# Seven half-size products for eight in an MLP down projection, and a place for each piece of w_mod

## What is computed

```python
m = jax.nn.silu(c) @ w_mod + b_mod            # (1024) @ (1024, 6*1024): shifts, scales, gates sh1, sc1, g1, sh2, sc2, g2
h = rmsnorm(x, g_attn) * (1.0 + sc1) + sh1    # the context tokens likewise, from c_ctx
...
x = x + g1 * (mix @ w_out)
h = rmsnorm(x, g_mlp) * (1.0 + sc2) + sh2     # (1024 tokens, 1024)
a = jax.nn.relu(h @ w_mlp1)                   # w_mlp1 (1024, 4096): the up product
x = x + g2 * ((a * a) @ w_mlp2)               # w_mlp2 (4096, 1024): the down product
```

## Time and profile before

| what | value |
|---|---|
| median of 3 runs | 1471.31 us (1468.08 to 1471.95) |
| profiled execution, own time | 1470.41 us |
| its span, and granted clock | 1468.6 us, 0.984 |
| TensorE, VectorE, ScalarE, GpSimd busy | 96%, 57%, 42%, 27% |
| chain that ended last | TensorE 77%, VectorE 10%, ScalarE 8%, DMA 2% |

### The profile page before, as it was taken

The page is one execution under the profiler, slowest core; times in us unless marked ns, Lnnn a source line. Parts: engine busy times, 40 slices in busy tenths (PEclk is TensorE's granted clock), DMA queues, the critical chain, the costliest instruction groups (busy, mean ns, idle before and its releaser), DMA issues.

```text
span 1468.6 us, 19191 instructions
## 1 busy us (share of the span) xinstructions
PE 1403.3 (96%) x7466; PEld 1184.4 (81%) x7466; DVE 837.4 (57%) x1183; ACT 610.7 (42%) x1195; POOL 390.5 (27%) x263
## 2 busy tenths in 40 slices
PE   4799998899999999999999999999999999999998
PEld 0588887788788998988888888888888888888887
DVE  0677787788887877775775344352433524344342
ACT  1565655777777777972223121130301203021120
POOL 1465654000099991501101111020101102011010
PEclk7799998999999999999999999999999999999999
DMA  8546647900156546201132011020201102021113
GB/s 315 195 125 173 177 145 232 305 18 1 35 179 205 183 125 182 67 1 58 44 101 73 28 58 58 29 86 0 86 29 57 57 29 86 0 80 34 33 40 115
DMA packets 117203, 141.04 MB, mean 96 GB/s; under 512 B 7928, under 2 KB 98936, under 8 KB 114320
## 3 DMA queue, kind: packets, MB, share of 16 engines
q1 hardware_dynamic: 116880, 140.08, 30.5%
q0 software_dynamic: 256, 0.05, 0.0%
HBM read 108.37 MB, written 31.74 MB: 95 GB/s over the span
## 4 chain that ended last, share of the span: by engine, by line
PE 77%; DVE 10%; ACT 8%; DMA 2%; issue 2%; POOL 0%; SPq 0%; DVEq 0%; ACTq 0%; POOLq 0%
PE f_ps L2080 23%; PE f_ps L2073 22%; PE a_ps L1378 7%; PE o_ps L1733 6%; PE a_ps L1394 5%; PE a_ps L1422 4%; PE t_ps L940 3%; ACT s_pr L1473 2%; ACT s_pT L1483 2%; PE t_ps L929 2%; DVE s_nmx L1556 1%; PE t_ps L955 1%; DMA t_wm<-in_w_mod 1%; ACT l_pr L1490 1%; DVE l_nb L1561 1%
## 5 line engine op out<-in xcount | busy, mean ns | idle before, releaser
L2080 PE MATMUL f_ps<-f_w,f_aT 128*128 128x512 f32 x1536 | 351.8, 390 | 0.7
L2080 PEld LDWEIGHTS f_ps<-f_w,f_aT 128*128 128x128 f32 x1536 | 287.7, 188 | 63.5 <-DVE mix L2056 3.6
L2073 PE MATMUL f_ps<-h,f_w 128*128 128x512 f32 x1440 | 327.8, 389 | 0.5 <-DVE f_w L1931 0.5
L2073 PEld LDWEIGHTS f_ps<-h,f_w 128*128 128x128 f32 x1440 | 270.2, 188 | 56.9 <-DVE f_w L1931 0.9
L1983 POOL TENSOR_TENSOR f_w2r<-f_w2r,f_g 128x1024 f32<-128x1024 f32 x32 | 81.0, 2531 | 604.4 <-DMA f_w2r<-in_w_mlp 604.4
L2056 DVE TENSOR_TENSOR mix<-mix,f_ps 128x512 f32<-128x512 f32 x112 | 72.0, 684 | 205.2 <-PE f_ps L2080 204.7
L2037 DVE TENSOR_TENSOR f_a<-f_r 128x1024 f32<-128x1024 f32 x32 | 59.6, 1864 | 183.8 <-ACT f_r L2013 183.8
L2000 ACT ACTIVATE f_w<-f_w2r 128x1024 fp32r<-128x1024 f32 x32 | 33.7, 1054 | 292.7 <-PE f_ps L2080 285.0
L1570 DVE TENSOR_TENSOR l_pT<-a_ps,l_pT 128x512 fp32r<-128x512 f32 (+1 forms) x192 | 109.0, 594 | 53.0 <-ACT l_pT L1483 52.9
L1378 PE MATMUL a_ps<-l_k,l_q 96*128 96x512 f32 (+1 forms) x576 | 136.5, 366 | 0.5 <-DVE l_mo L1591 0.5
L2013 ACT ACTIVATE f_r<-f_ps 128x1024 f32<-128x1024 f32 x32 | 32.9, 1029 | 228.3 <-PE f_ps L2073 219.6
(11 more groups left out here) (199 smaller groups left out, 1896.1 us busy)
## 6 DMA issues: line engine op xcount, KB each, us to landing
l_wg<-in_w_mod SPq DMA_DIRECT2D x8, 2048.0 KB, 8.1
f_w1r<-in_w_mlp SPq DMA_DIRECT2D x32, 512.0 KB, 4.1
f_w2r<-in_w_mlp SPq DMA_DIRECT2D x32, 512.0 KB, 4.5
t_wm<-in_w_mod SPq DMA_DIRECT2D x8, 1024.0 KB, 7.5
scratch_k<-t_kT SPq DMA_DIRECT2D x20, 384.0 KB, 4.5
l_k<-scratch_k SPq DMA_DIRECT2D x8, 960.0 KB, 10.1
scratch_q<-t_qT SPq DMA_DIRECT2D x16, 384.0 KB, 4.8
l_q<-scratch_q SPq DMA_DIRECT2D x8, 768.0 KB, 6.7
```

The lines of the kernel that those rows point to most:

```text
L2073: last = nc.tensor.matmul(ps[:, b + half, :], w1[:, slot, w, k, :], h2[x][:, k, half * BANK:(half + 1) * BANK], start=(k == 0 and i == 0), ...
L2080: last = nc.tensor.matmul(ps[:, DB[t % 2] + half, :], aT[x][:, f, t * P:(t + 1) * P], w2[w][:, f, half * BANK:(half + 1) * BANK], start=(f ...
```

## The change

**The down product.** A turn's product of 512 hidden columns is cut into halves along the tokens (rows, 512 each), the hidden columns and the output columns. Instead of the eight products of halves it makes seven, by the scheme of Strassen and Winograd, and takes sums and differences of halves as operands:

- VectorE forms two row sums of a (`row_sums`) and two differences (`difference`); GpSimd forms four differences of the gated w2 (`mix_weights`); ScalarE and VectorE split each of the 14 operands (`high`, `low`). Each of these works on 2 x 512 elements per partition.
- A product is four token tiles t of 2 x 3 matmuls (`product`). M1, M6, M7 and M4 go on in the same banks 4 to 7, M2 and then M5 and M3 in banks 0 and 1, two tiles each. After each tile `take` adds the bank to a region of `mix`: 28 additions a turn, for 16.
- The operands have two sets of buffers, so the split of a product waits until the one before the last is done (`free`). In the last turn there are three sets more, in the room that the up products leave.
- The up products are single halves of 24 matmuls (`up_next`), one between products, for the turn after. `a` has two buffers. ScalarE squares in place, and VectorE no longer squares. w2 is loaded in two pieces of 1 MB a turn. The loop is unrolled.

**The token stage.** Each of the 8 pieces of w_mod has a place of its own, `ident` is loaded ahead of them, and the first product no longer waits for it. The w_in weights `a0` wait for the first four products, since they are written over that place. x tile 1 is loaded and squared ahead of `a1`, and scaled ahead of the low part of w_kv; tile 2 is scaled earlier; `uq` is split in token tile 1 instead of 2.

```diff
-    WR = 3
-    wm = Z.room("L")("t_wm", [P, WR, 2 * D])
+    wm_in = {i: Z.room(at, skip)(f"t_wm{i}", [P, n, 2 * D]) for i, at, skip, n in ((0, "H", 0, 4), (4, "L", 0, 3), (7, "T", 9984, 1))}
+    wm = [wm_in[i][:, k - i, :] for k in range(KC) for i in (0, 4, 7) if 0 <= k - i < (4, 0, 0, 0, 3, 0, 0, 1)[i]]
...
         def load_wm(k):
-            if k >= WR:
-                sp.wait_ge(wm_used, k - WR + 1)
-            sp.dma_start(wm[:, k % WR, :], A["w_mod"][0, k * P:(k + 1) * P, 0:2 * D]).then_inc(wm_loaded[k % WR], 16)
+            sp.dma_start(wm[k], A["w_mod"][0, k * P:(k + 1) * P, 0:2 * D]).then_inc(wm_loaded[k], 16)
 
         def next_x(i):
             sp.wait_ge(emptied, slot["x1", i] + 1)
             load_x(i + 2)
 
         sp.dma_start(cc[:, :, :], A["c_cols"]).then_inc(c_loaded, 16)
-        for k in range(WR):
-            load_wm(k)
         sp.dma_start(ident[:, :], A["ident"]).then_inc(ident_loaded, 16)
-        for k in range(WR, KC - 2):
+        for k in range(KC - 2):
             load_wm(k)
         load_x(0)
         load_wm(KC - 2)
         load_wm(KC - 1)
         load_raw("a0")
+        load_x(1)
         load_raw("a1")
-        load_x(1)
...
+            if j == "a0":
+                act.wait_ge(wm_used, 4)
...
         high_weights("a0")
+        square_x(1, stx[:, 1:2])
         high_weights("a1")
         hi_fill("x0", 0)
         hi_fill("x1", 0)
-        square_x(1, stx[:, 1:2])
...
+        inverse_x(1)
         low_weights("a1")
-        inverse_x(1)
+        scale_x(1)
...
-        pe.wait_ge(ident_loaded, 16)
         pe.wait_ge(silu_ready, 1)
         for k in range(KC):
-            pe.wait_ge(wm_loaded[k % WR], 16 * (k // WR + 1))
+            pe.wait_ge(wm_loaded[k], 16)
             for j in range(4):
-                last = MM(ps[32 * j:32 * j + 32, UB, :], silu[:, k, :], wm[:, k % WR, j * BANK:(j + 1) * BANK],
+                last = MM(ps[32 * j:32 * j + 32, UB, :], silu[:, k, :], wm[k][:, j * BANK:(j + 1) * BANK],
                           start=(k == 0), stop=(k == KC - 1))
             last.then_inc(wm_used, 1)
+        pe.wait_ge(ident_loaded, 16)
...
+    UPB, XB, YB = (2, 4), 4, 0
+    M1, M2, M6, M5, M3, M7, M4 = range(7)
...
+    ROW, HIGH_D = {M1: 0, M2: 0, M6: 0, M5: 1, M3: 0, M7: 1, M4: 1}, {M1: 0, M2: 0, M6: 1, M5: 1, M3: 1, M7: 1, M4: 0}
+    bank_of = lambda i, t: XB + t if i in (M1, M6, M7, M4) else YB + t % 2
+    region_of = lambda i, t: (4 * ROW[i] + t, HIGH_D[i])
+    number = lambda d, i, t: NG * d + GROUPS.index((i, t))
+    ORDER = [(0, 0), (1, 0), (0, 1), (1, 1), (2, 0), (2, 1), (3, 0), (3, 1)]
...
+    def load_w2(d, fh):
+        if d:
+            sp.wait_ge(b_low, 7 * (d - 1) + (M4 if fh else M7) + 1)
+        f = 2 * fh
+        sp.dma_start(w2[:, f:f + 2, :], w2_dram[:, FC * d + f:FC * d + f + 2, :]).then_inc(w2_loaded[fh], 16)
...
+    def slot(d, i):
+        if d == NCH - 1:
+            return (1, 0, 2, 3, 4, 1, 0)[i]
+        return (7 * d + i) % 2
+
+    def free(eng, d, i):
+        if d == NCH - 1 and i in (M6, M5, M3):
+            eng.wait_ge(up_ready, 2 * NF)
+        elif d == NCH - 1 and i > M3:
+            eng.wait_ge(out_ready, NG * d + DONE[M1 if i == M7 else M2])
+        elif 7 * d + i > 1:
+            before = 7 * d + i - 2
+            eng.wait_ge(out_ready, NG * (before // 7) + DONE[before % 7])
...
+        load_w2(0, 0)
+        load_w2(0, 1)
+        for g in range(2, 6):
             load_w1(g)
+        for c in range(1, NCH):
+            load_w1(FC * c + 2)
+            load_w1(FC * c + 3)
+            if c < NCH - 1:
+                load_w1(FC * c + 4)
+            load_w2(c, 0)
+            if c < NCH - 1:
+                load_w1(FC * c + 5)
+            load_w2(c, 1)
...
+        def mix_weights(d):
+            made = 4 * d
+            pool.wait_ge(w2_gated, FC * d + 4)
+            pool.wait_ge(b_low, 7 * d + M1 + 1)
+            G.tensor_tensor(b_part(0, 0), b_part(0, 1), b_part(0, 0), ALU.subtract).then_inc(w2_mixed, 1)
+            pool.wait_ge(w2_mixed, made + 1)
+            free(pool, d, M6)
+            t2 = op_b[slot(d, M6)][2][:, :, :]
+            G.tensor_tensor(t2, b_part(1, 1), b_part(0, 0), ALU.subtract).then_inc(w2_mixed, 1)
+            pool.wait_ge(w2_mixed, made + 2)
+            pool.wait_ge(b_low, 7 * d + M2 + 1)
+            G.tensor_tensor(b_part(1, 0), b_part(1, 0), t2, ALU.subtract).then_inc(w2_mixed, 1)
+            G.tensor_tensor(b_part(0, 1), b_part(1, 1), b_part(0, 1), ALU.subtract).then_inc(w2_mixed, 1)
...
+        def w1_high(g):
             act.wait_ge(w1_loaded, g * 16 + 16)
...
+            act.wait_ge(up_ready, 2 * g - 2 if g > 3 else g + 1)
+            nc.scalar.activation(w1[:, g % 2, 0, :, :], w1r[:, :, :], ACT.Copy).then_inc(w1_hi, 1)
+
+        def rectify(c, n, f, half, b):
+            x = a[c % 2][:, f, half * HB:(half + 1) * HB]
+            act.wait_ge(up_ready, 8 * c + n + 1)
+            if n == 0 and c > 1:
+                act.wait_ge(a_low, 7 * (c - 1))
+            nc.scalar.activation(x, ps[:, b, :], ACT.Relu).then_inc(rect, 1)
+            act.wait_ge(rect, 8 * c + n + 1)
+            nc.scalar.activation(x, x, ACT.Square).then_inc(a_ready, 1)
+
+        def high(d, i):
+            s = slot(d, i)
+            free(act, d, i)
+            if i in HALF:
+                act.wait_ge(a_ready, 8 * d + 8)
+            else:
+                act.wait_ge(a_mixed, 4 * d + {M5: 1, M6: 2, M3: 3, M7: 4}[i])
+            nc.scalar.activation(op_a[s][0][:, :, :], a_source(d, i), ACT.Copy).then_inc(a_hi, 1)
+            if i in (M1, M2, M3):
+                act.wait_ge(w2_gated, FC * d + (2 if i == M1 else 4))
+            else:
+                act.wait_ge(w2_mixed, 4 * d + {M5: 1, M6: 2, M4: 3, M7: 4}[i])
+            nc.scalar.activation(op_b[s][0][:, :, :], b_source(d, i), ACT.Copy).then_inc(b_hi, 1)
+
+        for n, (f, half) in enumerate(ORDER):
+            if f == 2 and half == 0:
+                w1_high(2)
+                w1_high(3)
+            if f == 3 and half == 0:
+                w1_high(4)
+            rectify(0, n, f, half, UPB[f % 2] + half)
+        high(0, M1)
...
+        def row_sums(d):
+            dve.wait_ge(a_ready, 8 * d + 8)
+            dve.wait_ge(a_low, 7 * d + M1 + 1)
+            s1, s2 = a_part(d, 0, 1), a_part(d, 0, 0)
+            V.tensor_tensor(s1, s1, a_part(d, 1, 1), ALU.add).then_inc(a_mixed, 1)
+            dve.wait_ge(a_mixed, 4 * d + 1)
+            V.tensor_tensor(s2, s1, s2, ALU.subtract).then_inc(a_mixed, 1)
+
+        def difference(d, i):
+            free(dve, d, i)
+            dve.wait_ge(a_mixed, 4 * d + 2)
+            V.tensor_tensor(a_source(d, i), a_part(d, 1, 0 if i == M3 else 1), a_part(d, 0, 0), ALU.subtract).then_inc(a_mixed, 1)
+
+        def take(d, i, *tiles):
+            for t in tiles:
+                row, half = region_of(i, t)
+                n = number(d, i, t)
+                dve.wait_ge(out_ready, n + 1)
+                if (row, half) in written:
+                    dve.wait_ge(added, written[row, half])
+                x = acc[:, 4 * half:4 * half + 4, row * P:(row + 1) * P]
+                y = fin[:, 2 * row + half, :].rearrange("p (k c) -> p k c", c=P) if d == NCH - 1 and i in (M2, M3, M7, M4) else x
+                V.tensor_tensor(y, x, ps[:, bank_of(i, t), :].rearrange("p (k c) -> p k c", c=P), ALU.add).then_inc(added, 1)
+                written[row, half] = n + 1
...
+        w1_low(2)
+        w1_low(3)
+        w1_low(4)
+        low(0, M1)
+        for c in range(1, NCH):
+            d = c - 1
+            low(d, M2)
+            w1_low(FC * c + 1)
+            row_sums(d)
+            take(d, M1, 0, 1, 2, 3)
+            low(d, M6)
+            take(d, M2, 0, 1)
+            w1_low(FC * c + 2)
+            take(d, M2, 2, 3)
+            low(d, M5)
+            take(d, M6, 0, 1, 2, 3)
+            difference(d, M3)
+            low(d, M3)
+            take(d, M5, 0, 1)
+            w1_low(FC * c + 3)
+            take(d, M3, 0, 1)
+            take(d, M5, 2, 3)
+            difference(d, M7)
+            low(d, M7)
+            if c < NCH - 1:
+                w1_low(FC * c + 4)
+            take(d, M3, 2, 3)
+            low(d, M4)
+            take(d, M7, 0, 1, 2, 3)
+            low(c, M1)
+            take(d, M4, 0, 1, 2, 3)
+        d = NCH - 1
+        low(d, M2)
+        row_sums(d)
+        low(d, M6)
+        take(d, M1, 0, 1, 2, 3)
+        low(d, M5)
+        take(d, M2, 0, 1)
+        difference(d, M3)
+        low(d, M3)
+        take(d, M2, 2, 3)
+        difference(d, M7)
+        take(d, M6, 0, 1, 2, 3)
+        low(d, M7)
+        take(d, M5, 0, 1)
+        low(d, M4)
+        take(d, M3, 0, 1)
+        take(d, M5, 2, 3)
+        take(d, M3, 2, 3)
+        take(d, M7, 0, 1, 2, 3)
+        take(d, M4, 0, 1, 2, 3)
...
+        def product(d, i, *tiles):
+            s = slot(d, i)
+            pe.wait_ge(a_low, 7 * d + i + 1)
```

(40 more changed lines are left out.)

327 lines of the change are left out of this document (149 added, 178 removed).

## The result

The changed kernel takes **1435.6 us** (median of 4 runs, 1433.8 to 1439.2) against 1469.7 us (1467.8 to 1472.0) for the kernel before on the same chip: a ratio of 0.9771, 95% interval 0.9749 to 0.9793. The forecast was 1437 us, the range 1421 to 1457. The profiled execution has a span of 1434.3 us and took 1436.1 itself, so 34.3 us of span are to be explained.

The account below looks back on a forecast made before the run. The prediction took TensorE, busy 96% of the span, as the bound, so fewer MLP matmuls save time if operands are ready. Terms from -43.5 us for removed matmuls to +17 for the last turn sum to -34.1: 1437 us, range 1421 to 1457.

Parts of the forecast that it names:

- waits at the heads of turns: MLP, head of each turn: the down product's waits for additions into mix should go, -3.5 us.
- MLP start, stand: Start of the MLP: w1's third block stands behind four pairs of Relu and Square, so TensorE waits 3.5 us; +3.0 us.
- MLP start, clock: Start of the MLP: the clock may fall in the stand; about half of 2.7 us taken, +1.5 us.
- seven middle turns: MLP turns with up products: these cover the extra work, M2's bank free 1.6 to 3.4 us ahead; 0 us.
- last turn, waits: Last MLP turn, no up products: TensorE stands 12 to 13 us at M2's third tile, about 3 later; +17 us.
- last turn, clock: Last MLP turn: after the long stand the clock is lost, 2.7 us partly under VectorE's work; +2 us.
- token stage and what follows: Token stage: earlier w_mod -5.3 us, earlier x tile 1 scaling -2.7, clock kept -2; -10 us, bounds 5 to 14.
- the exclusion of VectorE and GpSimd: Shared SBUF port lock: the two engines exclude each other, PSUM reads aren't held; last turn 6.7 us longer.
- B: Rival: the last turn doesn't stall, so 19 us of stand and clock come back; 1418 us, chance 0.13.
- C: Rival: M2's third tile is late 2 to 3 us in each of seven turns; 1451 to 1458 us, chance 0.17.
- D: Rival: M2's third tile stands 4.3 us and loses 2.7 of clock in seven turns; 1486 us, chance 0.07.
- E: Rival: the token stage gives little, its earlier modulation absorbed by tables and weights; 1447 us, chance 0.15.

Follow-up runs that it names:

- e3: The changed kernel with ScalarE's copy of w1's third block ahead of the fourth rectify instead of behind it: 1431.2 us (0.9727).
- e7b: The changed kernel with three unread VectorE operations ahead of M2's first additions in each middle turn: 1435.8 us (0.9762).
- e7: The changed kernel with seven unread VectorE operations ahead of M2's first additions in each of the seven middle turns: 1484.1 us (1.0091).
- e6: The changed kernel with GpSimd's four mixes of the last turn cut to 8 columns of 512, M6's weights read unmixed: 1430.7 us (0.9730).
- e1: The kernel before with only the token stage changed, the MLP left as it was: 1460.7 us (0.9928).
- e9: e3 with VectorE's last-turn additions of M1 and M2's first two tiles ahead of the row sums and M6's lows, two banks kept: 1422.7 us (0.9668).
- e4: The changed kernel with four banks instead of two for M2, M5 and M3 in the last turn, no order changed: 1435.8 us (0.9763).
- e5: The changed kernel with the edits of e3 and e4 and another last-turn order, GpSimd's mix for M7 held back: 1420.8 us (0.9667).
- e2: The kernel before with only the MLP changed, the token stage left as it was: 1444.0 us (0.9813).
- e8: The changed kernel with w_mod's places and the ident load kept, the token stage's other moves taken back: 1438.1 us (0.9778).

## Why the prediction held, term by term

| term | predicted | measured, and from what |
|---|---|---|
| 192 matmuls fewer | -43.5 | -43.5: count 7466 to 7274, a period of 81.60 us (81.5) |
| waits at the heads of turns | -3.5 | -3.2: a turn took 87.44 us before and 384 x 0.2267 = 87.04 without them, times 8; none left (572.00 of 572 busy) |
| MLP start, stand | +3.0 | +4.1: half products to third block 21.1 us (780.56 - 759.42) against 17.1 |
| MLP start, clock | +1.5 | +2.8 in the profiled execution (0.2 to 2.9, e3) |
| seven middle turns | 0 | 0 |
| last turn, waits | +17 | +14.7: 13.5 of waits and 1.2 of resuming (1431.06 - 1376.65 for 28 tiles of 1.36) |
| last turn, clock | +2 | +1.7: behind the long stand eight matmuls took 3.55 us (1397.18 to 1400.73, 0.43 apart) for 1.81 |
| end | -0.6 | -0.7: 1434.3 - 1431.06, against 3.9 |
| token stage and what follows | -10 | -10.3 |
| sum | -34.1 | -34.4, against -34.3 of span |

*Right for the stated reason.* The place, the releaser and the order of the long stand in the last turn (predicted 15.5 us behind the last up product and 12 to 13 us long; it begins at 1385.9, 14.8 us behind the start of that product's Relu at 1371.1, and is 11.2 us long); the stand of 3.5 us at the start (3.55); the cover in the middle turns (1.6 to 3.4 us predicted; 2.1 and 3.5 in the trace, and e7b and e7 show it from both sides); the exclusion of VectorE and GpSimd (e6). Of the rivals, B fails by the stand itself, C and D by the dense window, E by e1 (10.0 us).

*What was luck.* The changed kernel's start of the MLP came out 2.4 us dearer than forecast and its last turn 2.6 us cheaper. Had only one of the two come out so, the time would have been 2 to 3 us further off, still inside 1430 to 1444.

*Sizes that were off.* The 3.6 us of the earlier trace rows stand in the row of the weight loads; the row of the matmuls beside it has 0.7, and what the turns lost is 3.2, by their period. At the start a wait of 0.65 us for the low part of `h` was missed. VectorE's low took 2.32 us there, beside GpSimd's gating of `w2` (759.91 to 770.35 us). The step "*I take about half, +1.5 us*" for the clock was a guess between 0 and 2.7; the executions show both ends. The last turn was 2.5 us too dear: the waits at M3 and M5's second pair were 1.5 us for 3, and the long stand 1 us shorter, because three operations were held by GpSimd for 5.2 us together, and not for 7.2 (nor for the 6.7 that the prediction also gives).

In the token stage the sum was right, and so were its parts up to the second x tile. The last piece of `w_mod` was there at 26.0 us, where 26.6 was expected. Ahead of the second x tile 4.3 us of waiting for GpSimd went, but inside that tile TensorE now waits 1.83 us for VectorE's `t_c`, so 2.5 us went ("*2 to 3 of these go*"). And the clock stayed up there. TensorE in the second x tile's w_kv product, and a window in it, before:

```profile
58.19 2.91 PE L968 MATMUL t_ps<-w_kv,t_c 128*128 128x512 f32 x6
...
58.20:60.80 2.60, 2.60 (x8) 2.12 (x7) 1.61 (x3) 2.34 (x4) 2.27 (x6) 0.50 0.00 0
```

and changed:

```profile
48.62 0.65 PE L932 MATMUL t_ps<-ident,t_x 128*128 128x128 f32 x4 [1.83 <-DVE t_c L721]
49.03 1.63 PE L971 MATMUL t_ps<-w_kv,t_c 128*128 128x512 f32 x6
...
49.00:50.70 1.70, 1.67 (x10) 1.07 (x8) 1.52 (x3) 1.38 (x2) 1.62 (x5) 1.00 0.00 0
```

With the x tile ahead of this product and the w_in product behind it that is 2.1 us, for the 2 that the prediction took. The prediction reads half clock "*from 55.5 us*"; by the trace it began at 55.1. In the first spread there was nothing to gain in this execution: it took 6.52 us against 6.62 before, while e1, with the same token stage, did it in 5.08. Then 2.0 us of wait came back: 0.8 at the next `t_z` and 1.2 at the third x tile (4.14 for the 2.97 of the kernel before):

```profile
70.11 1.09 PE L929 MATMUL t_ps<-ident,t_x 128*128 128x128 f32 x4 [2.97 <-POOL t_x L408]
```

The lead there is 70.11 - 61.55 = 8.6 us. Where the other 1.7 us up to the MLP's 10.3 come from wasn't followed.

*The step that would have failed.* I named the two banks as what makes M2 wait ("*the second product can use two banks only*"), and "*the two banks are a fact of the code*" as the reason against rival B. The place and the size were right, the cause half right: with two banks and another order (e9) M2's third tile doesn't wait, and with four banks and the old order (e4) the time is that of the changed kernel. What binds is that VectorE does 12 lows, four sums and its additions in an order in which the addition that TensorE needs next stands last.

*Open.* Why the clock fell behind the stand of 3.55 us in five of seven executions and not in the other two isn't settled. That a late second half of `w2` makes the 2 us at M1 rests on ten traces that agree; no kernel was made to try it. Why that half is late in some executions isn't known.

## What to carry to other kernels

A cheaper algorithm that trades TensorE work for VectorE work was worth its full count here where other TensorE work covered the extra operations, and lost a part where that cover ended: look first at the last turn and the first one. In an in-order queue write down what the waiting engine needs next and what stands ahead of it; here more banks only moved the wait, while another order took away 7 us of 13.5. Ask of each place how much delay it hides: here 3.4 us a turn cost nothing that the time shows, and 7.9 us turned a gain of 2.3% into a loss of 0.9%. And before a wait in one trace is put down to an edit, look for it in the traces of kernels without that edit, as with the 2 us at M1.

## What the runs showed of the hardware

What a stand costs in clock isn't the same in each execution, and it doesn't grow with the stand. Behind one of 3.55 us at the same place the next 120 matmuls took from 27.5 us (twice) to 30.2 us in seven profiled executions. In the MLP a wait of 1.38 us cost no clock (e7b), one of 2.32 us cost 1.7 us (e5), and one of 4.36 us cost 2.5 us in the mean of six turns (e7). Behind 11.2 us it was 1.7 us in the changed kernel, 2.5 in e2 and 2.8 in e3, e7b and e8.

GpSimd is held by VectorE as well: in e3 one mix of 128x1024 took 2.40 us beside additions that read PSUM, and the next 3.25 us beside two lows. Additions of one PSUM and one SBUF operand took 2.47 us for four beside a mix of GpSimd (e9) and without one (e6).
